# A two-layer hybrid trunk with its layer loop written out, and the last layer's work for a next layer left out

## What is computed

```
mod = silu(c) @ w_ada[l] + b_ada[l]              # six vectors of 1024 per sequence
hn  = rmsnorm(x, norm1_g) * (1 + sc1) + sh1
xl, gl, bs, cs, hs = split(hn @ w_in, 5)         # 512 columns each
lru_out = rglru(gates of conv4(xl)) * gelu(gl)
sc_out  = bs * conv3(cs * hs)
x = x + g1 * (concat(lru_out, sc_out) @ w_out)
hn2 = rmsnorm(x, norm2_g) * (1 + sc2) + sh2
u, v = split(hn2 @ ffn_w_up, 2)                  # 2816 columns each
x = x + g2 * ((gelu(conv3(u)) * v) @ ffn_w_down)
```

## Time and profile before

| | us |
|---|---|
| median of 3 runs | 1389.32 (1389.26, 1389.32, 1392.93) |
| span of the profiled execution | 1388.3 |
| PE busy | 1337.3 |
| DVE busy | 704.9 |
| ACT busy | 470.1 |
| POOL busy | 52.0 |

### The profile page before, as it was taken

How to read it: one execution, slowest core, us unless ns; L and a number is a source line. 1 busy time by engine, 2 the same in 40 slices (tenths; PEclk the granted TensorE clock), 3 DMA queues, 4 the chain that set the end, 5 groups by cost and what they waited for, 6 DMA issues and landing times.

```text
span 1388.3 us, 24750 instructions
## 1 busy us (share of the span) xinstructions
PE 1337.3 (96%) x9795; PEld 1265.5 (91%) x9795; DVE 704.9 (51%) x1218; ACT 470.1 (34%) x591; POOL 52.0 (4%) x102
## 2 busy tenths in 40 slices
PE   5799999999999999999979999998999999999998
PEld 3698888799999999999969888888999999999997
DVE  2763663475533544355566168337554345434556
ACT  3523653252312332123343256226322223222332
POOL 2000000000000000000020000000000000000001
PEclk7899999999999999999989999998999999999999
DMA  9545655512222212221242655661222122122113
GB/s 318 174 152 170 208 199 182 182 61 92 80 71 92 91 60 91 91 73 64 79 136 89 209 178 184 208 222 38 92 91 91 61 91 91 61 91 91 64 62 119
DMA packets 110869, 166.60 MB, mean 120 GB/s; under 512 B 3688, under 2 KB 101961, under 8 KB 103622
## 3 DMA queue, kind: packets, MB, share of 16 engines
q1 hardware_dynamic: 102309, 113.61, 24.7%
q0 software_dynamic: 8320, 51.86, 11.1%
q10 hardware_dynamic: 160, 0.05, 0.0%
HBM read 162.51 MB, written 2.99 MB: 119 GB/s over the span
## 4 chain that ended last, share of the span: by engine, by line
PE 92%; DVE 3%; DMA 2%; issue 1%; ACT 1%; SPq 0%; DVEq 0%; POOLq 0%; ACTq 0%
PE ps L345 29%; PE ps L347 28%; PE ps L346 28%; PE ps L404 4%; DMA ada_w<-in_w_ada 1%; PE ps L490 1%; PE ps L427 1%; DMA work<-in_x_prompt 1%; DVE work L811 1%; DMA work<-in_w_ada 0%; DVE w_raw L1166 0%; PE ps L368 0%; PE ps L419 0%; DVE work L833 0%; PE ps L370 0%
## 5 line engine op out<-in xcount | busy, mean ns | idle before, releaser
L345 PE MATMUL ps<-norm_hi,w_hi 128*128 128x288 f32 x2048 | 612.7, 299 | 14.6 <-DVE norm_lo L784 13.8
L346 PE MATMUL ps<-norm_lo,w_hi 128*128 128x288 f32 x2048 | 606.7, 296 | 0.0
L347 PE MATMUL ps<-norm_hi,w_lo 128*128 128x288 f32 x2048 | 604.5, 295 | 0.0
L345 PEld LDWEIGHTS ps<-norm_hi,w_hi 128*128 128x128 f32 x2048 | 386.6, 189 | 34.4 <-issue 33.5
L347 PEld LDWEIGHTS ps<-norm_hi,w_lo 128*128 128x128 f32 x2048 | 388.0, 189 | 0.0
L346 PEld LDWEIGHTS ps<-norm_lo,w_hi 128*128 128x128 f32 x2048 | 387.3, 189 | 0.0
L345 PE MATMUL ps<-mid_hi,w_hi 128*128 128x288 f32 x904 | 269.3, 298 | 0.0
L346 PE MATMUL ps<-mid_lo,w_hi 128*128 128x288 f32 x904 | 266.7, 295 | 0.0
L347 PE MATMUL ps<-mid_hi,w_lo 128*128 128x288 f32 x904 | 265.8, 294 | 0.0
L774 DVE TENSOR_TENSOR w_lo<-w_raw,w_hi 128x2048 fp32r<-128x2048 f32 x93 | 213.0, 2290 | 94.8 <-ACT w_hi L547 94.6
L547 ACT ACTIVATE w_hi<-w_raw 128x2048 fp32r<-128x2048 f32 x93 | 177.7, 1910 | 165.2 <-PE ps L347 164.5
(11 more groups left out here) (189 smaller groups left out, 867.2 us busy)
## 6 DMA issues: line engine op xcount, KB each, us to landing
ada_w<-in_w_ada POOLq DMA_DIRECT2D x48, 1024.0 KB, 5.2
w_raw<-in_ffn_w_up SPq DMA_DIRECT2D x44, 1024.0 KB, 5.1
w_raw<-in_w_in SPq DMA_DIRECT2D x21, 1024.0 KB, 5.2
w_raw<-in_ffn_w_down SPq DMA_DIRECT2D x16, 1024.0 KB, 5.0
w_raw<-in_w_out SPq DMA_DIRECT2D x8, 1024.0 KB, 4.9
w_raw<-in_ffn_w_down SPq DMA_DIRECT2D x8, 768.0 KB, 4.2
work<-in_w_ada SPq DMA_DIRECT2D x4, 1024.0 KB, 11.3
work<-in_x_prompt SPq DMA_DIRECT2D x4, 512.0 KB, 5.3
```

What stands on the lines that cost most here:

```text
L345: T.matmul(out, WH[:, r, k, c:c + P], xh[:, k, h, :], start=start, stop=False)
L346: T.matmul(out, WH[:, r, k, c:c + P], xl[:, k, h, :], start=False, stop=False)
L347: last = T.matmul(out, WL[:, r, k, c:c + P], xh[:, k, h, :], start=False, stop=stop)
```

## The change

- The five loops over l become Python loops, so the code of each layer is written out once per layer, with constants for semaphore values and addresses. The inner loops over q stay.
- Round i = 2 is made only for l < L - 1 (`ada_rounds`): in the last layer its eight loads on POOL, its eight slices on PE, the `ada_rows` on ACT, the `ada_turn` on PE and the `modulation` on DVE are gone, and so are the waits for them.
- In the last layer the load of block PL on SP and its split on ACT and DVE are gone; SP waits for lo_done at L * PL + 2 ahead of final_g.
- In the last layer the copies into `BNEXT` and `CUR` and the two steps of `gains` are gone on DVE.
- `Steps` is not rebased any more and counts on through both layers.

The diff, without repeats of the same substitution:

```
+        def ada_rounds(l):
+            return ((l, 1), (l, 2), (l + 1, 0))[:3 if l < L - 1 else 2]
...
-            with sp.Fori(0, L) as l:
-                load(l * PL + 1, 1, a["w_in"][bass.ds(l, 1), :, 256:512])
+            for l in range(L):
+                load(l * PL + 1, 1, a["w_in"][l:l + 1, :, 256:512])
...
-                after = l * -1 + (L - 1)
-                load(l * PL + n, 0, a["w_in"][bass.ds(after, 1), :, 0:256])
-
-            sp.wait_ge(lo_done, L * PL + 3)
+                if l < L - 1:
+                    load(l * PL + n, 0, a["w_in"][l + 1:l + 2, :, 0:256])
+
+            sp.wait_ge(lo_done, L * PL + 2)
...
-            with pool.Fori(0, L) as l:
+            for l in range(L):
...
-                after = l * -1 + (L - 1)
-                for i, (lr, r) in enumerate(((l, 1), (l, 2), (after, 0))):
+                for i, (lr, r) in enumerate(ada_rounds(l)):
...
-            with pe.Fori(0, L) as l:
+            for l in range(L):
                 pe.wait_ge(mod_ready, l * 3 + 1)
...
-                    if k == 0:
-                        pe.wait_ge(ada_rows_ready, l * 3 + (i + 1))
-                    ada_slice(l * 24 + (8 + 8 * i + k), k)
+                    if i < len(ada_rounds(l)):
+                        if k == 0:
+                            pe.wait_ge(ada_rows_ready, l * 3 + (i + 1))
+                        ada_slice(l * 24 + (8 + 8 * i + k), k)
...
                 norm_stats(l * 2 + 2, 0)
-                pe.wait_ge(ada_rows_ready, l * 3 + 4)
+                pe.wait_ge(ada_rows_ready, l * 3 + len(ada_rounds(l)) + 1)
                 norm_stats(l * 2 + 2, 1)
...
-                    if g == 0:
+                    if g == 0 and l < L - 1:
                         ada_turn(l * 3 + 4)
...
-                        pe.wait_ge(mod_ready, l * 3 + 4)
+                        if l < L - 1:
+                            pe.wait_ge(mod_ready, l * 3 + 4)
...
-            with act.Fori(0, L) as l:
+            for l in range(L):
...
                 square(l * 18, KX)
-                ada_rows(l * 3 + 4)
+                if l < L - 1:
+                    ada_rows(l * 3 + 4)
                 std(l * 2 + 2)
...
-                            if m == 5:
+                            if m == 5 and l < L - 1:
                                 split(l, PL)
...
-            with dve.Fori(0, L) as l:
-                step.base, step.n = l * DVE_STEPS + before, 0
-                after = l * -1 + (L - 1)
+            for l in range(L):
...
-                step(V.tensor_copy(BNEXT[:], VEC[:, bass.ds(after, 1), 0:16].rearrange("p o n -> p (o n)")))
+                if l < L - 1:
+                    step(V.tensor_copy(BNEXT[:], VEC[:, l + 1, 0:16]))
...
-                    if g == 0:
+                    if g == 0 and l < L - 1:
                         modulation(l * 3 + 4, MOD_SH1, BNEXT[:])
...
-                        step(V.tensor_copy(CUR[:], VEC[:, bass.ds(after, 1), :].rearrange("p o n -> p (o n)")))
-                        dve.wait_ge(mod_ready, l * 3 + 4)
-                        gains(MOD_SC1, V_N1)
+                        if l < L - 1:
+                            step(V.tensor_copy(CUR[:], VEC[:, l + 1, :]))
+                            dve.wait_ge(mod_ready, l * 3 + 4)
+                            gains(MOD_SC1, V_N1)
...
-                            if m == 5:
+                            if m == 5 and l < L - 1:
                                 split(l, PL)
...
-                assert step.n == DVE_STEPS, step.n
-            step.base, step.n = L * DVE_STEPS + before, 0
```

More of the change, by code:

```diff
@@ L258, in _ @@
                     for s in range(2):
-                        load(l * PL + n, s, a["w_in"][bass.ds(l, 1), :, c0 + 256 * s:c0 + 256 * s + 256])
+                        load(l * PL + n, s, a["w_in"][l:l + 1, :, c0 + 256 * s:c0 + 256 * s + 256])
                         n += 1
                 for j in range(4):
-                    load(l * PL + n, j % 2, a["w_out"][bass.ds(l, 1), :, 256 * j:256 * j + 256])
+                    load(l * PL + n, j % 2, a["w_out"][l:l + 1, :, 256 * j:256 * j + 256])
                     n += 1
@@ L267, in _ @@
                             load(l * PL + q * 2 + (n + s), s,
-                                 a["ffn_w_up"][bass.ds(l, 1), :, bass.ds(q * 256 + (8 * g * P + s * DFF), 256)])
+                                 a["ffn_w_up"][l:l + 1, :, bass.ds(q * 256 + (8 * g * P + s * DFF), 256)])
                     n += K
@@ L271, in _ @@
                         load(l * PL + n, j % 2,
-                             a["ffn_w_down"][bass.ds(l, 1), 8 * g * P:(8 * g + K) * P, 256 * j:256 * j + 256])
+                             a["ffn_w_down"][l:l + 1, 8 * g * P:(8 * g + K) * P, 256 * j:256 * j + 256])
                         n += 1
                 assert n == PL
-                after = l * -1 + (L - 1)
-                load(l * PL + n, 0, a["w_in"][bass.ds(after, 1), :, 0:256])
-            sp.wait_ge(lo_done, L * PL + 3)
+                if l < L - 1:
+                    load(l * PL + n, 0, a["w_in"][l + 1:l + 2, :, 0:256])
+            sp.wait_ge(lo_done, L * PL + 2)
             sp.dma_start(FGB, a["final_g"].rearrange("(u n) -> u n", u=1).broadcast_to([P, D])).then_inc(fg_in, 16)
@@ L315, in _ @@
                     for q in range(2):
-                        src = a[w][bass.ds(l, 1)].rearrange("o (c q) i j -> q i (o c) j", q=2)[q]
+                        src = a[w][l:l + 1].rearrange("o (c q) i j -> q i (o c) j", q=2)[q]
                         pool.dma_start(BLK[q * HD:(q + 1) * HD, m, :, q * HD:(q + 1) * HD], src).then_inc(blk_full, 16)
-                after = l * -1 + (L - 1)
-                for i, (lr, r) in enumerate(((l, 1), (l, 2), (after, 0))):
+                for i, (lr, r) in enumerate(ada_rounds(l)):
                     with pool.Fori(0, KX) as k:
@@ L324, in _ @@
                 for name, i, r, n, r0 in NSO:
-                    dst = o["new_" + name][bass.ds(l, 1)]
+                    dst = o["new_" + name][l:l + 1]
                     dst = dst.rearrange("o b (c p) -> (o b c) p", p=P) if len(dst.shape) == 3 else \
@@ L950, in _ @@
             step(V.memset(CIN[1][:, 0:PADS], 0.0))
-            before = step.n
-            with dve.Fori(0, L) as l:
-                step.base, step.n = l * DVE_STEPS + before, 0
-                after = l * -1 + (L - 1)
+            for l in range(L):
                 split_half(l * 2 + 1, l, 1, 0)
@@ L1171 @@
 UP_STEPS = 6
-DVE_STEPS = 184
 _OUT = ["y_prompt", "y_sample", "new_lru_h_p", "new_lru_conv_p", "new_sc_conv_p", "new_ffn_conv_p",
```

## The result

Four runs of the changed kernel had a median of 1371.47 us (1370.70 to 1372.66) against 1389.29 us for the kernel before, run beside it. The recorded ratio is 0.9863, 95% interval 0.9844 to 0.9883, which corresponds to 1370.3 us; the quotient of the two medians alone is 0.9872. The forecast was 1374.5 us, with a range of 1371 to 1379.5. The profiled execution has a span of 1369.0 us, 19.3 us less than before; 14.8 were forecast.

A forecast was written before the change was run, and what follows sets the result against it. PE, busy for 96% of the span, was taken to bound the kernel; 8.3 + 5.4 + 0.6 + 0.43 + 0.1 = 14.8 us off 1389.3 us gave 1374.5 us, range 1371 to 1379.5.

The forecast's parts named there:

- Seam: Between layers 0 and 1: without the loop's jump the engines' late first instructions go, 5.4 us saved, bounds 3.8 and 5.7.
- Slices: Output projection of layer 1: seven unused conditioning slices inside PE's stream go, 1.18 us each, 8.3 us, bounds 7 and 8.6.
- rival (b): Output-projection tiles of layer 1, freed of slices, wait for weights or DVE, 0.9 us at each of seven: 1380.8 us; chance 0.05.
- Middle norm: Norm in the middle of layer 1: without ACT's copy of a slice's result the spread starts 0.6 us sooner, bounds 0 and 1.0.
- turn: After layer 1's first up group: PE no longer transposes the new rows into columns, 0.43 us saved, bounds 0.3 and 0.5.
- end: End of the kernel: of 4.2 us of weight split on ACT and DVE, 0.1 us is gained, bounds 0 and 0.2.
- Numbers in place of registers: Constant semaphore values: nothing gained on PE; small pieces in DVE and ACT chains at the norms, 1 us kept for the range.
- the start: Span up to the first product of layer 0: the prediction gave it no term.
- the room for the clock: Half-clock stretches at the seam and layer 1's middle norm may vanish or double: 1.4 us either way apiece, 2.8 us together.
- (a): Rival at the seam: PE's hole is first use of the code, not the jump, and stays: 1379.9 us; chance 0.06.
- (c): Rival: inner loops over q pay 3.8 us per fetched jump back on PE, slower, 1397 us if six are paid; chance 0.03.
- (d): Rival, whole kernel: PE's stalls are refilled by an unseen limit, time stays 1389 us; chance 0.02.

The follow-up runs named there:

- e3: The kernel before with its five loops over l written out on all engines and nothing dropped: 1383.22 us, ratio 0.9951.
- e5 to e7: The kernel before, loop over l written out on PE alone (ratio 0.9978), on all but PE (0.9994), on PE and ACT (0.9987).
- e2: The changed kernel again, no edit: 1375.20 us, ratio 0.9887 to the kernel before.
- e4: The changed kernel with layer 1's spare load, split, copies and gains put back, only the conditioning round dropped: 1376.06 us, ratio 0.9889 to the kernel before.
- e13: The changed kernel a fourth time, no edit: 1375.84 us, ratio 0.9901 to the kernel before.
- e1: The kernel before again, no edit: 1389.44 us, ratio 1.0006.
- e9: The changed kernel a third time, no edit: 1375.28 us, ratio 0.9894 to the kernel before.
- e12: The changed kernel with the inner loops over q on PE, ACT and DVE written out too: 1374.18 us, ratio 0.9886 to the kernel before.
- e8: The changed kernel with idle products added on PE in the norms: 1368.61 us, ratio 0.9854 to the kernel before.
- e14: e8 again, in one job with e13: 1367.54 us, ratio 0.9844 to the kernel before.

## Why the prediction was right or wrong

The table takes spans and stretches of PE from two profiles of the kernel before and four of the changed kernel; "from to" is the range over the profiles.

| stretch | before | after | mean gain | forecast |
|---|---|---|---|---|
| start of the span to the first product of layer 0 | 52.0, 50.2 | 49.9 to 52.7 | 0.0 | 0 |
| from there to the last product of layer 0 | 653.9, 655.2 | 653.5 to 654.3 | 0.6 | 0 |
| seam, last to first product | 15.0, 15.0 | 8.8 to 10.2 | 5.5 | 5.4 |
| from there to the last tile before the middle norm | 217.9, 218.0 | 209.2 to 210.4 | 8.3 | 8.3 |
| middle norm of layer 1 | 10.2, 10.0 | 9.0 to 10.0 | 0.8 | 0.6 |
| from there to the last product | 425.6, 425.8 | 424.7 to 426.0 | 0.5 | 0.43 |
| last product to the end | 13.8, 13.8 | 13.6 to 15.8 | -0.6 | 0.1 |
| span | 1388.3, 1387.9 | 1369.0 to 1375.6 | 15.0 | 14.8 |

**Seam.** Right in place; in size 5.5 us in the mean and 6.1 in the first profile, for 5.4. The jump was the cause (e3), and each engine paid for its own (e5 to e7). The sum had put L833 at 712.1, 1.9 us behind the end of L825, by a second half of the spread of 1.75 us at half clock. In the first profile L826 comes 1.36 us after L818 ends: that half took 1.27 us, and L773, the counterpart of L780, ended last. In e2 the whole spread runs at half clock and the seam gains 4.8 us.

**Slices.** Right: 8.4 us from the turn to the last product (53.50 to 45.06), and no new limit took their place (PE is busy for 43.00 of 43.00 us in the window above); rival (b) falls.

**Middle norm, turn, end.** The middle norm and the turn are right within 0.2 us in the mean. In the first profile the middle norm gained 1.2 us, more than the 1.0 I had given as its bound. The bound I drew from ACT's table load is where the stage now ends. At the end the split was worth 0.2 us (e4), yet the mean loses 0.6: in e2 and e13 half clock covers 6.8 and 4.5 us of this stretch, against 1.8 in the first profile. That this loss and the 0.6 us won in layer 0, neither of them forecast at that size, cancel is luck in the 15.0 us.

**Numbers in place of registers.** Nothing to measure in whole times. The gap ahead of the first product of a norm fell from 3.40 us to 3.22 us at the seam, a piece of 0.2 us, within the 1 us that I had kept for all such pieces.

**The steps that failed: the start, put at nothing, and the room for the clock.** The first ratio corresponds to 1370.3 us, below the range of 1371 to 1379.5. The mechanism stands, two sizes do not. The first profile gained 4.5 us more than the sum's 14.8: 2.1 ahead of the first product of layer 0, 0.7 at the seam, 0.6 in the middle norm, 0.5 behind it, 0.4 in layer 0, 0.2 in the stretch with the slices and 0.1 at the end.

The start had no term and no room; I had taken it from a single profile. One of the first conditioning slices waits there for its transfer of w_ada, here in the kernel before, in the changed kernel and in e1:

```profile
41.15 1.64 PE L404 MATMUL ps<-work,silu_c 128*32 128x512 f32 x8 [4.43 <-DMA work<-in_w_ada]
```

```profile
39.21 1.79 PE L394 MATMUL ps<-work,silu_c 128*32 128x512 f32 x8 [3.77 <-DMA work<-in_w_ada]
```

```profile
39.05 1.93 PE L404 MATMUL ps<-work,silu_c 128*32 128x512 f32 x8 [4.47 <-DMA work<-in_w_ada]
```

The first product of layer 0 follows this slice by 10.7 to 11.2 us in five of the six profiles of the two kernels (11.8 in e13). So 1.9 of the 2.1 us are a transfer that came sooner, and it comes sooner or later in the kernel before just as well.

For the clock I let one stretch in each of two stages vanish or double, 1.4 us apiece, beside 1.6 us one way for the spread at the seam. Half clock in fact moves in all four norms and over the final transposes. Behind the first product of layer 0 it lasts 28.8 us in the first profile, 34.1 in e9, 39.3 in e13 and 45.4 in e2, and that part of the span takes 1319.1, 1320.9, 1322.7 and 1325.1 us: 0.36 us for each us of half clock, 6.0 us in all. The 20 runs say the same: the three with a mean granted clock of 0.981 have spans of 1369.0 to 1369.4 us, the eight with 0.976 or less 1373.6 to 1376.2 us. The kernel before spreads by 5.5 to 10 us in the four jobs too, which three runs did not show. So the range of 1371 to 1377.5 for the likeliest case was too narrow: single runs lie from 1370.65 to 1377.91 us. That the forecast of 1374.5 lies 0.6 us from the median of all 20 runs is what its terms are worth, with the luck named above.

**What stays open.** Why the clock was high in all of the first four runs: 0.979 to 0.981, which only two of the 16 later ones reached (1370.65 and 1373.53 us). The first profile is 5.5 us shorter than the mean of the three later ones: 1.6 us at the start, 0.75 at the seam, 0.4 in the middle norm, 0.6 in layer 0, 1.0 in the rest of layer 1, 1.0 at the end. No instruction differs; chance or chip was not settled.

**Rivals.** (a) was refuted by e3, (b) by the trace. (c) did not occur: no hole at an inner jump, and e12 gained nothing clear by removing them. (d), no change in time, falls with the measured times. The Trainium skill, "Runtime: NRT & Kernel Launch", section "Instruction fetch mechanics", says that code is fetched ahead in sequence, and that a taken branch to a page not held makes the engine wait for that page. The traces agree: the instruction transfers at the seam are there with the jumps and gone without them. The same section of the Trainium skill says that each engine's sequencer fetches through a queue of its own. For PE the trace agrees (q8); the transfers that go with ACT's and DVE's loops all stand in q14, and the holes of 4.9 (PE), 3.9 (ACT) and 2.95 us (DVE) were found apart in e5 to e7.

## What to carry to other kernels

Where an outer loop's jump falls on a chain between engines, write the loop out on every engine of that chain: each has its own hole, they hide one another, and PE alone brought 2.2 of the 6.1 us at the seam. Work beside a full PE stream is worth only what the next arrival leaves uncovered (0.2 of 4.2 us here), while seven slices inside the stream were worth their full length. Before giving a range, look at how many runs there are, at what the clock does in every gap and at which transfer the start waits for. Idle products can hold the clock for a comparison, but check in both traces that they hold up no real one.

## What was not expected of the hardware

- 81 idle products of 128 columns on PE in the gaps kept the granted clock at 1.00 across the seam (e8) and were worth 8.3 us in one job (e14 beside e13; 0.991 over the span of the profiled run, 0.976 without them).
- At a jump back over a whole layer the trace shows the instruction transfers themselves, and PE starts 1.65 to 1.72 us after the last of them ahead of it has landed.
- The same program had spans from 1369.0 to 1375.6 us in four profiles. Of the 6.6 us between these two, 6.0 go with 16.6 us more of half clock behind the first product, and 0.5 lie ahead of it.
- The same cure brought the kernel before only 2.9 us (1389.52 to 1386.62). At its seam the clock fell all the same and the idle products then held up the first product by 2.0 us. That the 5 us hole let the clock fall is likely but not shown by itself, since these kernels also lacked the 3 idle products that e8 has ahead of the spread.
